# A two-layer hybrid transformer step on one core: work moved inside the projections, the dense blocks and the routing

## The reference

```python
for l in range(2):                       # for each stream
    sh1, sc1, gt1, sh2, sc2, gt2 = split(silu(cond) @ w_ada[l] + b_ada[l], 6)
    h = rmsnorm(x, norm_mix_pre[l]) * (1 + sc1) + sh1
    y = mixer(h)      # h @ w_in[l] (2400 wide), four attention groups A, B, C, D, then @ w_o[l];
                      # latent queries and keys are rotated (2-D RoPE), C has two latent norms
    x = x + gt1 * rmsnorm(y, norm_mix_post[l])
    h = rmsnorm(x, norm_ffn_pre[l]) * (1 + sc2) + sh2
    f = swiglu(h) if l == 0 else top2_of_8_experts(h)      # 2816 wide; 8 x 3584 wide
    x = x + gt2 * rmsnorm(f, norm_ffn_post[l])
```

## Time and profile before

| | us |
| --- | --- |
| median of three runs | 1704.3 |
| the profiled execution | 1709.76 |
| its span in the profile | 1708.0 |
| PE busy in the span | 1609.8 |
| DVE busy | 1203.2 |
| ACT busy | 964.6 |
| start of the expert loop's first gather | 674.54 |

### The profile page before, as it was taken

How to read it: one execution, slowest core, us unless ns; L and a number is a source line. 1 busy time by engine, 2 the same in 40 slices (tenths; PEclk the granted TensorE clock), 3 DMA queues, 4 the chain that set the end, 5 groups by cost and what they waited for, 6 DMA issues and landing times.

```text
span 1708.0 us, 23134 instructions
## 1 busy us (share of the span) xinstructions
PE 1609.8 (94%) x8263; PEld 1327.0 (78%) x8263; DVE 1203.2 (70%) x1041; ACT 964.6 (56%) x917; POOL 90.0 (5%) x142
## 2 busy tenths in 40 slices
PE   5989879999898887999999999999999999999996
PEld 3857769998686767888888888888888888888884
DVE  2456444443636643888988988988988888888885
ACT  3333334333533341777677777677677776776773
POOL 2420040000011010000000000000000000000001
PEclk7998899999998985999999999999999999999998
DMA  9854374566752443898998998998998998998991
GB/s 371 260 186 151 122 212 162 197 200 239 258 192 92 143 139 115 297 367 317 365 371 319 360 372 316 362 371 318 363 368 318 366 366 316 369 364 324 362 365 42
DMA packets 218290, 473.85 MB, mean 277 GB/s; under 512 B 8464, under 2 KB 41536, under 8 KB 218240
## 3 DMA queue, kind: packets, MB, share of 16 engines
q1 hardware_dynamic: 215024, 466.38, 76.6%
q0 software_dynamic: 3216, 6.79, 1.4%
HBM read 470.62 MB, written 2.52 MB: 277 GB/s over the span
## 4 chain that ended last, share of the span: by engine, by line
PE 90%; DVE 5%; ACT 2%; issue 1%; DMA 1%; POOL 1%; SPq 0%; POOLq 0%; DVEq 0%; ACTq 0%
PE ps L1528 22%; PE ps L1529 22%; PE ps L1533 22%; PE ps L1543 3%; PE ps L1550 3%; PE ps L1544 3%; PE ps L1913 2%; PE ps L1742 2%; PE ps L1573 2%; PE ps L1706 2%; PE ps L1925 1%; PE ps L1585 1%; PE ps L1616 1%; DMA raw<-in_w_ada 1%; DVE region L1092 1%
## 5 line engine op out<-in xcount | busy, mean ns | idle before, releaser
L1044 DVE TENSOR_TENSOR w_lo<-raw,w_hi 128x2048 fp32r<-128x2048 f32 (+1 forms) x397 | 903.5, 2285 | 189.9 <-ACT w_hi L716 189.4
L716 ACT ACTIVATE w_hi<-raw 128x2048 fp32r<-128x2048 f32 (+1 forms) x397 | 758.1, 1914 | 256.9 <-PE ps L1529 236.7
L1528 PE MATMUL ps<-w_hi,x_hi 128*128 128x512 f32 (+1 forms) x1216 | 439.1, 372 | 9.0 <-issue 6.3
L1529 PE MATMUL ps<-w_hi,x_lo 128*128 128x512 f32 (+1 forms) x1216 | 430.3, 365 | 0.0
L1533 PE MATMUL ps<-w_lo,x_hi 128*128 128x512 f32 (+1 forms) x1216 | 285.1, 364 | 0.0
L1528 PEld LDWEIGHTS ps<-w_hi,x_hi 128*128 128x128 f32 x1216 | 230.8, 190 | 49.6 <-issue 11.8
L1529 PEld LDWEIGHTS ps<-w_hi,x_lo 128*128 128x128 f32 x1216 | 230.7, 190 | 36.1
L1533 PEld LDWEIGHTS ps<-w_lo,x_hi 128*128 128x128 f32 x1216 | 207.3, 188 | 39.6
L1528 PE MATMUL ps<-w_hi,h_hi 128*128 128x512 f32 x528 | 208.2, 394 | 0.0
L1529 PE MATMUL ps<-w_hi,h_lo 128*128 128x512 f32 x528 | 207.8, 394 | 0.0
L1533 PE MATMUL ps<-w_lo,h_hi 128*128 128x512 f32 x528 | 141.6, 393 | 0.0
(11 more groups left out here) (241 smaller groups left out, 1263.9 us busy)
## 6 DMA issues: line engine op xcount, KB each, us to landing
raw<-in_moe_w_gate SPq DMA_DIRECT2D x112, 1024.0 KB, 5.2
raw<-in_moe_w_up SPq DMA_DIRECT2D x112, 1024.0 KB, 5.3
raw<-in_moe_w_down SPq DMA_DIRECT2D x112, 1024.0 KB, 5.3
raw<-in_w_ada SPq DMA_DIRECT2D x48, 1024.0 KB, 6.1
raw<-in_w_in SPq DMA_DIRECT2D x20, 960.0 KB, 9.9
raw<-in_ffn_w_gate SPq DMA_DIRECT2D x11, 1024.0 KB, 5.5
raw<-in_ffn_w_up SPq DMA_DIRECT2D x11, 1024.0 KB, 7.2
raw<-in_ffn_w_down SPq DMA_DIRECT2D x11, 1024.0 KB, 5.1
```

The costliest lines, as they stand in the source:

```text
L716: act.activation(split_hi(c, slice(0, width(c))), raw[:, r % NRAW, 0:width(c)], ACT.Copy).then_inc(hi_done, 1)
L1044: dve.tensor_sub(split_lo(c, n), raw[:, raw_of(c) % NRAW, n], split_hi(c, n)).then_inc(lo_done, 1)
L1528: pe.matmul(out, xh, split_hi(c, w), start=start, stop=False, skip_group_check=True)
L1529: last = pe.matmul(out, xl, split_hi(c, w), start=False, stop=False, skip_group_check=True)
```

## The change

1. `columns` takes four matmuls by 4 columns in place of eight by 2; `section` reads them in the new order.
2. In the input projection DVE rotates the A columns after block 1, the B columns after block 2, and KPE and the two latent norms after block 3; ACT's `c_sq` moves to blocks 3 and 4.
3. Dense FFN: no hardware loop; `columns(0, 5)` stands in block 0, a half of a stream's gate rows in each of the blocks 1 to 4.
4. `norm_h`: DVE applies the first four pieces, ACT the last four.
5. A fourth pair of split buffers for the FFN's second unit, which is split earlier; other turns of the slots.
6. Routing: logits and row transposes of stream 0, then `columns(1, 5)`, stream 1's `norm_T`, stream 0's gates, and then stream 1.
7. DVE's second residual before layer 1 waits for POOL's root of stream 0. The memset of the accumulators stands before the wait for ACT's exponentials.

```diff
 def slot(c):
     if c < 9:
         return (c + 2) % 3
-    if c == 9 or c == win_u(1, NWIN) - 1:
+    if c == 9:
         return 0
-    return c % 3 if c < win_u(1, NWIN) else (c + 1) % 3
+    if c == FFN_U + 1:
+        return 3
+    if c <= FFN_U:
+        return c % 3
+    return (c + 2) % 3 if c < win_u(1, NWIN) else -c % 3
...
+            def norm_h(l, which, s):                       # ACT
...
+                for k in range(4, KT):
...
+                    last = act.activation(h[:, P * k:P * k + P], src, ACT.Identity, bias=mod[:, l, 3 * which, k, s:s + 1], scale=scale)
...
             def columns(l, k):                             # PE
...
-                for kt in range(KT):
-                    sel = C_SEL + 2 * (kt // 4)
-                    last = pe.matmul(col_ps(l, k)[:, 2 * kt:2 * kt + 2], mrow[:, m % 2, P * (kt % 4):P * (kt % 4) + P],
-                                     cst[:, sel:sel + 2], start=True, stop=True)
+                for kt in range(4):
+                    last = pe.matmul(col_ps(l, k)[:, 4 * kt:4 * kt + 4], mrow[:, m % 2, P * kt:P * kt + P],
+                                     cst[:, C_SEL:C_SEL + 4], start=True, stop=True)
...
+                    if j == 1:                             # DVE, after block j of the projection
+                        dve.wait_ge(win_evac[1], NWIN * l + 2)
+                        link(rope(proj[1][:, QA:QA + 384], 6, 64))
...
+                def block(c, f):                           # PE, dense FFN
...
+                    if f == 0:
+                        columns(0, 5)
+                    if 1 <= f <= 4:
+                        pe.wait_ge(gbs, f + 3)
+                        gates(0, 1, (f - 1) // 2, (f - 1) % 2, 1)
...
-                split_to(wo_u(l, 2) + 1)                   # ACT, end of a layer's mixer
+                act.wait_ge(out_ctx[l], NOUT)
+                split_to(wo_u(l, 2) + 2 - l)
                 post_half(l, 0, 1)
                 norm_sq(l, 1, 0)
                 norm_scale(l, 1, 0)
                 post_half(l, 1, 1)
+                norm_h(l, 1, 0)
                 if l == 0:
                     norm_hi(l, 1, 0)
-                split_to(wo_u(l, 2) + 2)
                 norm_sq(l, 1, 1)
+                if l:
+                    rows(l, 5)
                 norm_scale(l, 1, 1)
-                rows(l, 5)
+                if l == 0:
+                    rows(l, 5)
+                norm_h(l, 1, 1)
...
-            split_to(MOE_U + 3)
+            split_to(MOE_U + 2)
```

More of the change, by code:

```diff
@@ L493, in load @@
                         ffn_d(r % NRAW, f - 1)
[L495 to L507 removed]
+            for r in range(MOE_R):
                 load(r)
@@ L1292, in route @@
                 dve.tensor_sub(dm, m2, m1).then_inc(r_diff, 1)
-                split_to(MOE_U + 3)
+                for s in range(2):
+                    last = dve.memset(acc[s], 0.0)
+                last.then_inc(m_h, 1)
                 dve.wait_ge(r_exp, 1)
```

282 lines of the change are left out of this document (131 added, 151 removed).

## The result

The changed kernel takes 1674.54 us (median of 4 runs, 1673.86 to 1676.77) where the kernel before took 1704.05 beside it: a ratio of 0.9823, 95% interval 0.981 to 0.9835. The gain is 29.5 us; the prediction had 18, and its range ended at 1677. The sign was right and the size was outside the range. The profiled execution took 1674.89 us, its span 1673.1, which is 34.9 less than the span of before; that execution of before was 5.7 us above its median and the one of after 0.4 above, so some 5 of the 34.9 are chance.

The account below looks back on a forecast made before the run. PE bounds the expert loop, so all gains lie ahead of the first gather: 22.35 us ahead of the last norm, less 4.3 in the routing, gives 18, hence a median of 1686 us; range 1677 to 1697.

Parts of the forecast that it names:

- The columns: In the column sections: records by 4 columns cost the same as by 2, gaining 4.5 us; bounds 0 and 5.4.
- The bound of 5.4: Upper bound in us on the gain from shorter column sections, if the covers leaked nothing.
- The start: At the kernel's start: the first split begins 1.25 us earlier, gaining 1.25 us; bounds 0 to 2.
- Rotation and latent norms: In both input projections: PE's transposes come earlier, gaining 2.4 us in layer 0 and 4.0 in layer 1, sum 6.4.
- The dense head: Between FFN norm and block 0: columns and gates move into the blocks, gaining 7.9 us; bounds 5 and 9.
- The norms: At layer 0's FFN norm a gain of 1.2 us, at layer 1's first norm 1.1.
- Routing: From layer 1's last norm to the first gather: new order loses 4.3 us; bounds 2 us earlier and 8 later.
- the sentence that kept the clock low: In the new routing: same kinds of work and longer pauses, so PE's granted clock stays at the lower level, 0.50.
- its rival: In the expert loop: units' first products meet their splits late, making the kernel slower; 0.1 us a unit gives 1720; chance 0.06.

Follow-up runs that it names:

- the filled attention: Changed kernel with PE products of no use ahead of its waits at the end of both attentions: 1668.41 us.
- ten fillers there: Kernel before with ten products of no use put on PE ahead of its waits in the routing: 1705.72 us against 1704.97.
- the one with fillers in its sections: Changed kernel with two products of no use, 128x128 by 512 columns, ahead of the eight records of each section: 1692.01 us.

## Why the prediction was wrong

*The columns* are the term that failed. It had 4.5 us, and some 2 to 3 more stood in the terms of the start, the dense head and the routing; undone they are 17.0, 15.4 by the second measurement. Their part on PE's path was seen rightly in kind: 9.4 us of records less 7.1 that waits give back is 2.3, so the covers hid more than I took and not less. What I left out is the clock, which stands between its two levels in both attentions and in the routing: with the longer sections 10.5 us more were lost to the half clock in the profile. The bound of 5.4 was no bound: it priced only the records, and not all of those, since the term's eight sections by 0.92 are 7.4.

*The clock in general.* The sum had 1.3 us for it, at block 0. The half clock cost 55.3 us ahead of the experts before and 34.3 after. Work and idle time together fell by 12.1 us, where the sum without its 1.3 has 16.7: apart from the clock the change gave less than I said, and the clock gave all of the surplus, even if all 5 us of chance are taken off it. The rows had it in the open: the granted clock in layer 0's attention and in layer 1's was 0.90 and 0.88 before. I asked for each edit what it hides behind, and not at which clock what follows would run.

*The start* came out at 2.0 us against 1.25: the first product at 36.55, for 38.56. No run holds this firm: it is 36.99 in the second profile of the changed kernel and 38.15 in the one with the norms on DVE, which does not touch the start.

*Rotation and latent norms*: 7.1 undone against 6.4. The sum is right partly by luck, as layer 0 gave 3.6 for the 2.4 said and layer 1 2.8 for 4.0. *The dense head*: 5.8 against 7.9, inside its bounds; a block with a gate step took 17.88 us and one without 16.99, so 0.9 each where 0.98 was said. *The norms*: 1.6 and 1.0 in their passages against 1.2 and 1.1, right, and the same pieces cost as much or more further on, so the edit as a whole shows no gain.

*Routing* was to lose 4.3 us and lost 0.9 up to the gather. Its mechanism stood step by step: a pause for the router (9.59, said about 9, with a load of 7.1 us in place of 6.4), then L712 behind L765 and L1060 behind L712, 7.29 us of pause (said 7.3). What failed is the sentence that kept the clock low: it came back behind the second pause, and the half clock cost 6.0 us there in place of 12.6. The gather started at 642.01, outside the 655 to 662 that I gave: 11 us of it because the passages ahead gave 33.4 us and not 22.35, and 3.4 in the routing. Of the Trainium skill's rule (page TensorE: Matmul & The Clock Gate, section on the HAM clock gate), by which the clock rises after a sustained busy stretch, I had said that this stretch of before does not agree with it. The row stands, 6.86 of 6.90 us busy at 0.50. But the rows of the filled attention agree with the rule, since a fuller PE ran the transposes in 1.04 us and not 1.91; read as a direction it was a better guide than the one row against it.

*The slots* of the dense blocks were not in the sum: 2.7 us in the blocks of the profile, 1.0 in the medians, within their scatter. *The expert loop* kept its 126 us, and its rival fell.

Added up, undone one by one: 17.0 + 7.1 + 5.8 + 1.0 = 30.9 against the 29.5 measured. That they meet is partly luck. Taken from 1676.16 the four make 24.5 against 28.5; the new order of the routing was never undone, DVE's pause behind the experts stands in none of the four, and each of them moves the clock of what follows.

## What to carry to other kernels

Where a profile shows a granted clock below 1 in a passage that PE bounds, price an edit there twice, once by the time it takes off PE's path and once by the clock of what follows, and take the wider range. Find the pauses of a microsecond or two ahead of long work first: an early load (14.2 us here) or a few products of no use in front of a wait (6.1 us) are cheap to try. But measure the whole kernel each time: a pause of 6.5 us that went in the routing gave nothing at all, and neither did ten fillers there. When two profiles are compared, look behind the last loop too: 2.3 us were gained there without an edit.

## What the runs showed of the hardware

- PE's clock is part of the scatter. The changed kernel's medians were 1674.54 and 1676.16; the one with fillers in its sections spread over 10 us (1687.24 to 1697.42) and the one with the norms on DVE as well (1670.16 to 1680.19), each with one program. The mean granted clock of the execution goes along: 0.971 at the low end of both, 0.968 and 0.964 at the high end.
- The pace of back-to-back products depended on how the three buffers of split weights were dealt out: up's 256 columns took 0.1165 us from slot 1 and 0.1203 from slot 2, down's 512 columns 0.2267 from slot 2 and 0.2327 from slot 0, at a granted clock of 1.00. It followed the slots when they were put back. It is not the slot that is read alone, since the gate unit's 256 columns took 0.1177 both from slot 1 and from slot 0. In the expert loop the turned slots changed nothing that the rows show.
- The same DVE instruction behind a branch not taken came after 2.63 to 2.76 us of idle time in five profiles and after 0.33 to 0.35 in fourteen, waiting for no semaphore.
- A change of ScalarE's table took 1.3 us in all at the head of the dense FFN of before: the copy ahead of it ended at 246.33 us, the load ran from 246.36 for 1.28, and SiLU began at 247.65.
- A product by 4 columns takes what one by 2 takes (253 and 251 ns); a product by 512 columns in fp32 shows as two records and takes 0.94 us (1.88 for two at the end of the filled attention), near twice the 0.5 that I had put into the expectations.
